# MLP up projection in seven quarter products for six of its eight chunks

## What is computed

```python
def squared_relu_mlp(h, w_up, w_down):          # h: 512 x 2048, w_up: 2048 x 8192, w_down: 8192 x 2048
    u = jax.nn.relu(jnp.einsum('bsd,df->bsf', h, w_up))
    return jnp.einsum('bsf,fd->bsd', u * u, w_down)
```

## Time and profile before

| | |
|---|---|
| time, median of 3 runs | 2876.81 us (2875.32 to 2878.39) |
| span of the profiled execution | 2873.9 us |
| TensorE busy in the span | 2837.2 us |
| up projection, first to last matmul | about 1535 to 2250 us |

### The profile page before, as it was taken

The page is one execution under the profiler, slowest core; times in us unless marked ns, Lnnn a source line. Parts: engine busy times, 40 slices in busy tenths (PEclk is TensorE's granted clock), DMA queues, the critical chain, the costliest instruction groups (busy, mean ns, idle before and its releaser), DMA issues.

```text
span 2873.9 us, 38425 instructions
## 1 busy us (share of the span) xinstructions
PE 2837.2 (99%) x14896; PEld 2372.4 (83%) x14896; DVE 1653.3 (58%) x1699; ACT 1060.7 (37%) x1155; POOL 405.2 (14%) x438
## 2 busy tenths in 40 slices
PE   8999999999999999999999999999999999999997
PEld 5888777788899988898888888888888888888886
DVE  7545777755454433534534433333343798888888
ACT  5433433423453322332424322323233333333334
POOL 4000000000001132200011233233233200000001
PEclk9999999999999999999999999999999999999999
DMA  5333232233357764423423555556556755556555
GB/s 166 97 85 87 75 82 63 68 91 81 107 145 233 218 201 121 176 88 105 145 74 88 165 184 186 177 174 195 179 166 203 270 219 219 208 215 218 205 211 132
DMA packets 453647, 439.80 MB, mean 153 GB/s; under 512 B 9104, under 2 KB 365488, under 8 KB 453424
## 3 DMA queue, kind: packets, MB, share of 16 engines
q1 hardware_dynamic: 424288, 344.56, 39.1%
q0 software_dynamic: 29264, 93.90, 9.2%
HBM read 360.31 MB, written 75.50 MB: 152 GB/s over the span
## 4 chain that ended last, share of the span: by engine, by line
PE 89%; DVE 5%; ACT 2%; DMA 2%; issue 2%; POOL 0%; DVEq 0%; SPq 0%; ACTq 0%
PE slab_ps L867 18%; PE slab_ps L869 18%; PE slab_ps L868 18%; PE down_ps L1465 6%; PE down_ps L1467 6%; PE down_ps L1466 6%; PE mix_ps L869 2%; PE mix_ps L868 2%; PE mix_ps L867 2%; PE down_ps L867 2%; PE down_ps L869 2%; PE down_ps L868 2%; DVE dn_c L2246 1%; ACT w_hi L1491 1%; DMA w_raw<-in_w_in_dram 1%
## 5 line engine op out<-in xcount | busy, mean ns | idle before, releaser
L867 PE MATMUL slab_ps<-act_hi,w_hi 128*128 128x512 f32 (+2 forms) x2704 | 1022.6, 378 | 15.1 <-DVE act_lo L2148 11.2
L868 PE MATMUL slab_ps<-act_lo,w_hi 128*128 128x512 f32 (+2 forms) x2704 | 999.8, 370 | 0.0
L869 PE MATMUL slab_ps<-act_hi,w_lo 128*128 128x512 f32 (+2 forms) x2704 | 999.8, 370 | 0.0
L2096 DVE TENSOR_TENSOR w_lo<-w_raw,w_hi 128x2048 fp32r<-128x2048 f32 x200 | 469.2, 2346 | 370.7 <-ACT w_hi L1491 370.0
L867 PEld LDWEIGHTS slab_ps<-act_hi,w_hi 128*128 128x128 f32 (+1 forms) x2704 | 509.5, 188 | 109.6 <-issue 23.4
L869 PEld LDWEIGHTS slab_ps<-act_hi,w_lo 128*128 128x128 f32 (+1 forms) x2704 | 509.2, 188 | 87.9 <-issue 0.8
L868 PEld LDWEIGHTS slab_ps<-act_lo,w_hi 128*128 128x128 f32 (+1 forms) x2704 | 509.8, 189 | 85.0 <-issue 5.1
L1491 ACT ACTIVATE w_hi<-w_raw 128x2048 fp32r<-128x2048 f32 x200 | 381.9, 1910 | 476.1 <-PE slab_ps L869 359.8
L1465 PE MATMUL down_ps<-half_hi,u_slot 128*128 128x512 f32 x896 | 349.5, 390 | 0.8 <-DMA u_slot<-u_park 0.8
L1467 PE MATMUL down_ps<-half_lo,u_slot 128*128 128x512 f32 x896 | 349.5, 390 | 0.0
L1466 PE MATMUL down_ps<-half_hi,u_slot 128*128 128x512 f32 x896 | 349.3, 390 | 0.0
(11 more groups left out here) (418 smaller groups left out, 3092.4 us busy)
## 6 DMA issues: line engine op xcount, KB each, us to landing
w_raw<-in_w_mlp_up_dram SPq DMA_DIRECT2D x64, 1024.0 KB, 6.7
b<-in_w_mlp_down_dram SPq DMA_DIRECT2D x64, 1024.0 KB, 6.9
w_raw<-in_w_in_dram SPq DMA_DIRECT2D x56, 1024.0 KB, 5.6
u_slot<-u_park SPq DMA_DIRECT2D x112, 512.0 KB, 8.3
w_raw<-in_w_cross_kv_dram SPq DMA_DIRECT2D x32, 1024.0 KB, 6.3
u_park<-u_hi POOLq DMA_DIRECT2D x32, 896.0 KB, 9.0
u_park<-u_lo POOLq DMA_DIRECT2D x32, 896.0 KB, 8.9
w_raw<-in_w_mix_out_dram SPq DMA_DIRECT2D x16, 1024.0 KB, 5.8
```

Source lines behind the costliest of these rows:

```text
L867: mm(ps, wh, xh, start=first, stop=False)
L868: mm(ps, wh, xl, start=False, stop=False)
L869: return mm(ps, wl, xh, start=False, stop=last)
L2096: tt(w_lo[:, slot], w_raw[:, slot], f32(w_hi[:, slot]), ALU.subtract).then_inc(on["slab_lo"], 1)
```

## The change

Chunks 1 to 6 of the up projection (STC = 6, 24 pairs) are made in seven products in place of two windows a pair. A pair's weights are four quarters of 1024 x 128 (b11, b12, b21, b22), the activations four quarters of 1024 x 256.

- The activations' sums are made once, during chunk 0, on DVE (`left_parts`) and split by ACT and DVE (`left_hi`, `left_lo`) into `s1`, `s24` and the place of one of the quarters. That quarter is parked in DRAM (`left_park`, 2 MB in two DMAs) and loaded back by SP for the last chunk. `s24` lies over `main`, so `main` is parked in DRAM too (4 DMAs of 1 MB) and comes back in the last chunk, where the transposes and the two subtractions in `main` are made now.
- Each product is 8 x 3 matmuls of 256 columns. Products 0, 2, 4, 6 accumulate in one PSUM bank half (`joint`), 1 and 3 in another (`inner`), 5 in a third (`top`); between the products ACT copies the bank out (`part_out`), and DVE adds these copies up.
- Of the four sums of weight quarters a pair, DVE makes two (`first_weight_sum`, `second_weight_sum`) and POOL's queue two, as accumulating DMAs of 512 KB from SBUF to SBUF (`weight_sums`): b12 += b22 gives weight 4, t_raw += b21 gives weight 6. Seven split weights of 1024 x 128 go through a ring of four places.
- The four sums of the hidden values of these pairs are made by DVE (`hidden_sums`) instead of POOL.
- The loads of quarters are 512 KB each, written out for all pairs; `sum_hidden`, `hidden_square`, `hidden_hi`, `hidden_lo` swap their two buffers in the chunks that still use windows.

The core of the diff (left out: SP's first and last loads, the sums of the activations, the first and last chunk, and arguments of waits that only count):

```diff
+        quarter_act = lambda t, i, j: t[:, KT // 2 * j:KT // 2 * (j + 1), HS * i:HS * (i + 1)]
+        ring = lambda w, n: w[:, 1 - n % 4 // 2, n % 2 * (SLAB // 2):(n % 2 + 1) * (SLAB // 2)]
+        LEFT = ([quarter_act(t, 0, 0) for t in (act_hi, act_lo)], [s1[:, part] for part in range(2)],
+                [s24[:, 0, part] for part in range(2)], [s24[:, 1, part] for part in range(2)],
+                [quarter_act(t, 1, 0) for t in (act_hi, act_lo)], [quarter_act(t, 0, 1) for t in (act_hi, act_lo)],
+                [quarter_act(t, 1, 1) for t in (act_hi, act_lo)])
+        left_sum = t1[:].rearrange("p j (a t) -> p (j a) t", t=HS)
+        b11_raw, b22_raw, b21_raw = w_raw[:, 1, 0:SLAB // 2], w_raw[:, 0, 0:SLAB // 2], w_raw[:, 0, SLAB // 2:SLAB]
+        t_raw = ucomb[:, 1, 0:4].rearrange("p a t -> p (a t)")
+        b12_raw = (w_raw[:, 1, SLAB // 2:SLAB], ucomb[:, 1, 4:8].rearrange("p a t -> p (a t)"))
+        weight_raw = lambda n: (b11_raw, t_raw, t_raw, b22_raw, b12_raw[n // STN % 2], b21_raw, t_raw)[n % STN]
+        st_banks = lambda j: (M[j % 2][:, 0:HS], M[2 + j % 2][:, 0:HS], M[4 + j % 2][:, 0:HS])
...
+            def next_quarters(c, j):
+
+                src = quarter_of(c, j + 1, 0, 0)
+                sp.wait_ge(on["slab_lo"], c * (STN * HM) + (ST0 + STN * j + 1))
+                load_quarter(b11_raw, src, raw_in[1])
+                src = quarter_of(c, j + 1, 0, 1)
+                if past_first(c, j > 0):
+                    sp.wait_ge(on["slab_lo"], c * (STN * HM) + (ST0 + STN * (j - 1) + 5))
+                else:
+                    sp.wait_ge(on["u_lo_done"], HM - 1)
+                load_quarter(b12_raw[(j + 1) % 2], src, x_loaded[1])
+                src = quarter_of(c, j + 1, 1, 1)
+                sp.wait_ge(on["slab_lo"], c * (STN * HM) + (ST0 + STN * j + 5))
+                load_quarter(b22_raw, src, raw_in[0])
+                src = quarter_of(c, j + 1, 1, 0)
+                sp.wait_ge(on["slab_lo"], c * (STN * HM) + (ST0 + STN * j + 7))
+                load_quarter(b21_raw, src, x_loaded[0])
...
+                p = c * HM + (j + 1)
+                pool.wait_ge(st_sums, 2 * (p) + (SUMS0 - 1))
+                pool.wait_ge(x_loaded[1], 16 * p + 16)
+                pool.wait_ge(raw_in[0], 16 * p + RAW0)
+                pool.dma_start(b12_raw[j % 2], b22_raw, accum_op=ALU.add).then_inc(on["up_in"], 16)
+                pool.wait_ge(on["slab_lo"], c * (STN * HM) + (ST0 + STN * j + 3))
+                pool.wait_ge(x_loaded[0], 16 * p + 16)
+                pool.dma_start(t_raw, b21_raw, accum_op=ALU.add).then_inc(on["pos_in"], 16)
+
+            def next_pair(c, j, last=False):
+                park_hidden(c, HM - 1 + j)
+                if not last:
+                    weight_sums(c, j + 1)
...
+                joint, inner, top = st_banks(j)
+                for i in range(STN):
+                    n = STN * j + i
+                    pe.wait_ge(on["slab_lo"], c * (STN * HM) + (ST0 + n + 1))
+                    if i == 0 and past_first(c, j >= 2):
+                        pe.wait_ge(on["slab_out"], c * (STN * HM) + (ST0 + STN * j - STN))
+                    if i in (2, 3, 4, 6):
+                        pe.wait_ge(st_copied, c * (4 * HM) + (COPY0 + 4 * j + {2: 1, 3: 2, 4: 3, 6: 4}[i]))
+                    if isinstance(c, int) and c == 0 and j == 0:
+                        if i == 0:
+                            pe.wait_ge(on["x_rstd"], 2)
+                        if i in (1, 2, 3, 4):
+                            pe.wait_ge(on["act_ready"], i + (5 * KT))
+                    wh, wl = (ring(w, n).rearrange("p (k n) -> p k n", n=P) for w in (w_hi, w_lo))
+                    xh, xl = LEFT[i]
+                    bank = (joint, inner, joint, inner, joint, top, joint)[i]
+                    for k in range(KT // 2):
+                        first, end = k == 0 and i in (0, 1, 5), k == KT // 2 - 1
+                        mm(bank, wh[:, k], xh[:, k], start=first, stop=False, skip_group_check=True)
+                        mm(bank, wh[:, k], xl[:, k], start=False, stop=False, skip_group_check=True)
+                        last = mm(bank, wl[:, k], xh[:, k], start=False, stop=end, skip_group_check=True)
+                    last.then_inc(on["slab_mul"], 1)
...
+                if past_first(c, n >= 4):
+                    act.wait_ge(on["slab_mul"], c * (STN * HM) + (ST0 + n - 3))
+                if i in (0, 3, 5):
+                    act.wait_ge({0: raw_in[1], 3: raw_in[0], 5: x_loaded[0]}[i], 16 * p + (16 if i == 5 else RAW0))
+                elif i == 4:
+                    act.wait_ge(on["up_in"], 16 * p + 16)
+                elif i == 6:
+                    act.wait_ge(on["pos_in"], 16 * p + 32)
+                elif i == 1:
+                    act.wait_ge(st_sums, 2 * (p) + (SUMS0 - 1))
+                else:
+                    act.wait_ge(st_sums, 2 * (p) + (SUMS0 - 0))
+                fn(ring(w_hi, n), weight_raw(n), ACT.Copy).then_inc(on["slab_hi"], 1)
...
+                weight_hi(c, n + 3)
+                act.wait_ge(on["u_squared"], c * (2 * HM) + 2 * (HM + j))
+                part_out(c, n, urelu0[:, 0:HS], joint)
+                weight_hi(c, n + 4)
+                part_out(c, n + 1, urelu1[:, HS:S], inner)
+                weight_hi(c, n + 5)
+                part_out(c, n + 2, urelu1[:, 0:HS], joint)
+                weight_hi(c, n + 6)
+                act.wait_ge(on["u_summed"], c * HM + (HM + j))
+                act.wait_ge(on["u_hi_parked"], c * (16 * HM) + 16 * (HM - 1 + j))
+                fn(u_hi[:], ucomb[:, 0, 1:], ACT.Copy).then_inc(on["u_hi_done"], 1)
+                if not last:
+                    weight_hi(c, n + 7)
+                part_out(c, n + 4, urelu0[:, HS:S], joint)
+                if last:
+                    slabs.step(STN * PAIRS - 1)
+                    split_hi(NOT_SLABS, slabs.at(-1))
                     slabs.step()
+                else:
+                    weight_hi(c, n + 8)
+                    weight_hi(c, n + 9)
+                pair_square(c, j, 1)
+                pair_square(c, j, 0)
...
+                p = c * HM + (j + 1)
+                dve.wait_ge(raw_in[1], 16 * p + RAW0)
+                dve.wait_ge(x_loaded[1], 16 * p + 16)
+                if past_first(c, j > 0):
+                    dve.wait_ge(on["slab_lo"], c * (STN * HM) + STN * j + ST0)
+                else:
+                    dve.wait_ge(on["u_lo_done"], HM - 1)
+                tt(t_raw, b11_raw, b12_raw[j % 2], ALU.add).then_inc(st_sums, 1)
+
+            def second_weight_sum(c, j):
+
+                dve.wait_ge(raw_in[0], c * (16 * HM) + 16 * (j + 1) + RAW0)
+                dve.wait_ge(on["slab_lo"], c * (STN * HM) + (ST0 + STN * j + 2))
+                tt(t_raw, t_raw, b22_raw, ALU.add).then_inc(st_sums, 1)
...
+                weight_lo(c, n + 3)
+                weight_lo(c, n + 4)
+                hidden_sums(c, j)
+                weight_lo(c, n + 5)
+                weight_lo(c, n + 6)
+                dve.wait_ge(on["u_hi_done"], c * HM + (HM + j))
+                dve.wait_ge(on["u_lo_parked"], c * (16 * HM) + 16 * (HM - 1 + j))
+                tt(u_lo[:], ucomb[:, 0, 1:], f32(u_hi[:]), ALU.subtract).then_inc(on["u_lo_done"], 1)
+                product(3)
+                copied(3)
+                tt(urelu1[:, upper], inner, urelu1[:, upper], ALU.add).then_inc(on["slab_out"], 1)
+                if not last:
+                    first_weight_sum(c, j + 1)
+                    weight_lo(c, n + 7)
+                    weight_lo(c, n + 8)
+                    second_weight_sum(c, j + 1)
+                copied(4)
+                tt(urelu1[:, lower], urelu0[:, lower], urelu1[:, lower], ALU.add).then_inc(st_middle, 1)
+                dve.wait_ge(on["slab_out"], c * (STN * HM) + (ST0 + STN * j + 1))
+                dve.wait_ge(st_middle, c * HM + (MID0 + j + 1))
+                stt(out=urelu1[:], in0=urelu1[:], scalar=0.0, in1=rstd[:], op0=ALU.min, op1=ALU.mult).then_inc(
+                    st_relu, 1)
+                if last:
+                    slabs.step(STN * PAIRS - 1)
+                    split_lo()
                     slabs.step()
+                else:
+                    weight_lo(c, n + 9)
+                product(5)
+                tt(urelu0[:, upper], top, urelu0[:, upper], ALU.add).then_inc(on["slab_out"], 1)
+                dve.wait_ge(on["slab_out"], c * (STN * HM) + (ST0 + STN * j + 2))
+                stt(out=urelu0[:, upper], in0=urelu0[:, upper], scalar=0.0, in1=rstd[:, upper], op0=ALU.max,
+                    op1=ALU.mult).then_inc(st_relu, 1)
+                product(6)
+                stt(out=urelu0[:, lower], in0=joint, scalar=0.0, in1=rstd[:, lower], op0=ALU.max, op1=ALU.mult).then_inc(
+                    on["slab_out"], STN - 2)
```

More of the change, by code:

```diff
@@ L514, in _, with quarter_of @@
             slabs.leave(NT)
[L515 to L519, removed]
+            for j in range(MC):
```

(41 more changed lines are left out.)

233 lines of the change are left out of this document (194 added, 39 removed).

## The result

The changed kernel takes 2909.5 us (2907.5 to 2911.7), the kernel before 2876.2 beside it: a ratio of 1.0116, with a 95% interval of 1.0102 to 1.0130. It is slower by 33 us where 34 us less were forecast.

A forecast was written before the change was run, and what follows sets the result against it. TensorE was taken to stay the bound, at 20.2 us a pair: 2873.9 - 37.4 (24 pairs) + 3.4 (edges) = 2839.9, plus 2.9 from profiled span to median, 2842.8, said as 2843 us; range 2836 to 2864.

The forecast's parts named there:

- TensorE's price: TensorE's work per pair: seven products of 2.88 us, 20.16 us in place of 21.76.
- VectorE's 16.8 of 20.16: VectorE's work per pair, 16.8 us within TensorE's 20.16, so throughput allows the saving.
- the copies' slack: ScalarE's copies between products: copy 0 ends at 4.6 us against 5.76, 1.1 us of slack, cost 0.
- The loop: Pair's wait cycle through second accumulating DMA, ScalarE and VectorE: L + 12.1 us; TensorE stays the bound under L 8.1.
- Rival 3: Slower: the loop sets the pair past L = 9.5; at 10.0, pair 22.1, time 2888 us; chance 0.10.
- the edges: Chunk 0, first pair and return to full windows: 0, 0.4 and 3 us, 3.4 in the sum.
- L: Landing time of each pair's second accumulating DMA (t_raw += b21): 6 to 8.3 us, 7.2 in the middle.
- what is left to wait is 0 to 2.5 us: Second accumulation's wait for the first, issued some 5.7 us earlier and nearly or quite landed: 0 to 2.5 us.
- The DMA share: DMA engines' load in the pairs: 0.87 to 0.95 forecast; above 0.95 would show the forecast wrong.
- Chunk 0 at no cost: Activation sums, 32 us of VectorE, fit 47 us free in seven windows; two overrun by 1.0 and 1.3; cost 0.
- The return: Last chunk: parked quarter needed 11.2 us after the request, queued behind load and parks; cost 3 us, 0 to 6.
- The chance of slower: Probability given to the changed kernel being slower than the one before: 0.11, against 0.87 faster.

## Why the prediction was wrong, step by step

**What was right.** TensorE's price: forecast 20.16 us a pair, 20.09 where nothing else binds. VectorE's 16.8 of 20.16 (83%): 83%. No cost between products (the copies' slack) once the loop is out of the way. The loop itself, with the second accumulation in it and the same members behind it; its rest is 12.6 us and not 12.1, since the handovers cost 0.6 and not 0.1. The point where it decides is thus 7.5 us and not 8.1. Rival 3 described the mechanism, the condition and the sign, and its condition ("to wait behind both weight loads and the first accumulation") is the one that the runs found. Its price was too low: with 10.1 us in the pairs and its 3.4 at the edges it gives 2890 us, and the other 19 us are the edges.

**L, the mis-sized term.** Taken 7.2, measured 9.6. That cost 24 x (22.18 - 20.2) = 47.5 us, by far the most. The step that failed reads that the first accumulation "has then nearly or quite landed; what is left to wait is 0 to 2.5 us". The issues came about as forecast: from the park of u_hi to the second accumulation 9.3 us (forecast 9.3), from the first accumulation to the second 6.0 (5.7). But the first had 3.3 us left to land, since in this company it takes 8.7 to 10.5 us and not some 6, and the loads, which were placed in time ("the next loads at about 17") and charged nothing, had 5.6 and 7.2 left. The earlier trace rows already held a sign of it: a 1 MB load lands in 6.3 us alone and in 11.1 beside two parks, 4.8 more for 1.8 MB. On top of the 4.6 us of a join from an idle queue that makes 9.4. This is an estimate made afterwards, from 256 KB joins, and that it comes so close to 9.6 is in part luck.

**The DMA share.** I named 0.95 as the sign of trouble. The loop bound the kernel at 0.84 and was free of it at 0.89. A mean share says nothing of five transfers that go out within 10 us of each other.

**Chunk 0 at no cost; measured 13 us.** The step "seven windows with some 6.7 us free each, 47 us" counted two things that weren't there. The diff's steps lie in four windows, and of the free time of a window 3.7 us lie between the eviction and the low part, where VectorE waits for ScalarE and no step was placed. Further, the copy of the left sum on ScalarE stood ahead of the high part, which the count of VectorE's time doesn't show. The overrun was put at 1.0 and 1.3 us and came to 3.5 to 5.7 in each of three windows; TensorE stood 2.2, 4.5 and 1.9 us, and the clock behind the longest of these, which the forecast left out, cost some 2 more.

**The return, 3 us (0 to 6) forecast; 10.5 measured.** The gap is 6.7 us, and the clock behind it, which the forecast left out, costs 2.5 more (below). The quarter was needed 11.2 us after it was asked for, as forecast (2168.3 and 2179.5), and its second half landed 17.0 us after its issue. The sum of bytes was right in kind, but it let the quarter have its share in order; the parks of the last pair and 1 MB of slab shared the engines the whole time.

**The sum again.** This part of the kernel grew by 737.0 - 704.8 = 32.2 us: 10.1 in the pairs (forecast -37.4) and 22.1 at the edges (forecast 3.4). So 2842.8 + 47.5 + 18.7 = 2909.0, measured 2909.5. With L repaired alone it is 2858, above the forecast by the two edges though inside its range (2836 to 2864); with all three repaired it is 2837. The gain was there, and three orderings spent it. The chance of slower, 0.11, was too small: the earlier trace rows had 8.2 to 10.1 for the same operation in a burst, with no row that excluded a burst here.

## What to carry to other kernels

A transfer that an engine waits for in every round belongs ahead of the transfers that nobody needs yet, whatever queue these are on; size its landing by rows with the same company, and not by rows of an idle queue. Where work is moved into an engine's free time, ask where in the window that time lies and what stands at the head of the other engine's queue meanwhile: a sum of free microseconds is no place. And when a change loses while the bound engine's busy time fell, look for the few places where it stands; here a number in one wait, two statements swapped with a wait added, and some steps spread were worth 72 us.

## What the runs showed of the hardware

- An accumulating DMA of 512 KB within SBUF lands 4.4 us after issue when the two loads are out of its way (the first accumulation has 1.5 us left), and 9.6 behind 3.3 MB sent in the 9 us before it. In the same place a plain copy takes 8.3. Its issue holds GpSimd for 862 ns, that of the copy 569. The Trainium skill, "DMA: Bandwidth & Descriptors", section "Anatomy of one DMA — SWDGE (gpsimd) path", gives 3.2 us by its fit for 512 KB; the quiet time is 1.2 above that, and the busy one three times as long.
- A gap costs more than its length. Behind the 6.7 us gap at the last chunk matmuls of 512 columns start 0.43 us apart (the first two 0.59) until 2191.7 and 0.23 after that, and the granted clock of the next 6.8 us is 0.61 on average, so mostly at the 1.2 GHz level, then 1.00:

```profile
2186.43:2193.23 6.80, 6.80 (x19) 5.43 (x20) 0.00 (x0) 0.00 (x0) 0.00 (x0) 0.61 0.88 230
2193.30:2200.00 6.70, 6.70 (x31) 5.51 (x31) 2.79 (x2) 4.03 (x3) 0.24 (x1) 1.00 0.00 0
```

19 matmuls in 6.8 us, where 30 of 0.227 fit, are 2.5 us lost in addition. Behind the 4.5 us gap in chunk 0 it is the same (0.68 over 6.8 us, 21 matmuls). In the pairs the clock fell with nine of the gaps of 1.8 to 2.1 us, and not with all of them (see the loop).
